# Gathering token rows in four pieces and turning them on VectorE; gate and up weights as one 8 KB run per partition

## What is computed

```python
scores = sigmoid(hf @ w_router)                  # 64 experts, 8 chosen for a token, weights sum to 2.5
hp = concatenate([hf, zeros((1, dm))])           # pad row
def body(acc, blk):                              # a block is 128 (token, expert) pairs of one expert
    toks, bw, e = blk
    xb = hp[toks]
    yb = (silu(xb @ w_gate[e]) * (xb @ w_up[e])) @ w_down[e]
    return acc.at[toks].add(yb * bw[:, None]), None
```

## Time and profile before

| | us |
|---|---|
| three runs | 2484.62, 2490.03, 2492.65 |
| median | 2490.03 |
| profiled execution | 2485.66 |
| its span, first to last instruction | 2483.8 |
| TensorE busy in the span | 2382.5 (96%) |
| VectorE busy | 1575.5 (63%) |
| ScalarE busy | 1161.9 (47%) |
| GpSimd busy | 767.3 (31%) |

### The profile page before, as it was taken

The page is one execution under the profiler, slowest core; times in us unless marked ns, Lnnn a source line. Parts: engine busy times, 40 slices in busy tenths (PEclk is TensorE's granted clock), DMA queues, the critical chain, the costliest instruction groups (busy, mean ns, idle before and its releaser), DMA issues. The chain is left out here.

```text
span 2483.8 us, 49979 instructions
## 1 busy us (share of the span) xinstructions
PE 2382.5 (96%) x11840; PEld 1954.7 (79%) x11842; DVE 1575.5 (63%) x2285; ACT 1161.9 (47%) x1621; POOL 767.3 (31%) x829
## 2 busy tenths in 40 slices
PE   8899999989997799999999999999999999999986
PEld 6677777678886688888888888888888888888875
DVE  6686867768878756555665555656665556655447
ACT  4525253542225645445554445545554445544334
POOL 0010100011110134334543433534443334444327
PEclk9999999989998899999999999999999999999998
DMA  7242323364445579778988878888888789987863
GB/s 254 77 144 98 111 94 111 117 218 164 171 164 206 196 230 284 223 219 270 273 259 233 254 218 263 268 266 262 257 253 243 224 223 274 283 247 222 216 221 136
DMA packets 253808, 524.34 MB, mean 211 GB/s; under 512 B 18065, under 2 KB 165169, under 8 KB 249649
## 3 DMA queue, kind: packets, MB, share of 16 engines
q1 hardware_dynamic: 204464, 336.64, 39.7%
q0 software_dynamic: 48672, 186.86, 29.4%
q10 hardware_dynamic: 608, 0.02, 0.0%
HBM read 386.61 MB, written 136.87 MB: 211 GB/s over the span
## 5 line engine op out<-in xcount | busy, mean ns | idle before, releaser
L2503 PE MATMUL psG<-gu_split,xT_hi 128*128 x2624 | 624.3, 390 | 2.9 <-ACT xT_hi L2340 1.5
L2503 PEld LDWEIGHTS psG<-gu_split,xT_hi 128*128 128x128 f32 x2624 | 493.8, 188 | 106.2 <-issue 3.6
L2326 POOL DMA_INDIRECT acc<-y,si x162 | 290.1, 1791 | 728.6 <-DMA acc<-y,si 413.3
L2409 DVE TENSOR_TENSOR gu_split<-raw_gu,gu_split (+1 forms) x127 | 290.6, 2288 | 175.3 <-ACT gu_split L2344 171.7
L2514 PE MATMUL psG<-gu_split,xT_lo 128*128 x1304 | 339.3, 402 | 5.9 <-issue 5.8
L2514 PEld LDWEIGHTS psG<-gu_split,xT_lo 128*128 128x128 f32 x1304 | 233.1, 188 | 50.1 <-issue 8.7
L2344 ACT ACTIVATE gu_split<-raw_gu x126 | 234.3, 1907 | 33.5 <-issue 33.5
L2301 POOL DMA_INDIRECT xg<-htab,gi x164 | 205.0, 1250 | 130.4 <-POOL gi L2298 109.7
L2409 DVE TENSOR_TENSOR d_lo<-raw_d,d_hi (+1 forms) x64 | 146.7, 2292 | 149.5 <-ACT d_hi L2344 149.5
L2389 ACT ACTIVATE HT_hi<-psH 128x256 fp32r<-128x256 f32 x162 | 62.4, 385 | 351.6 <-PE psH L2521 351.6
L2406 DVE TENSOR_TENSOR xT_lo<-psX,xT_hi 128x512 fp32r<-128x512 f32 x328 | 209.7, 680 | 8.5 <-ACT xT_hi L2340 8.5
(11 more groups left out here) (388 smaller groups left out, 3723.7 us busy)
## 6 DMA issues: line engine op xcount, KB each, us to landing
raw_gu<-in_w_gate_dram SPq DMA_DIRECT2D x64, 1024.0 KB, 6.0
raw_gu<-in_w_up_dram SPq DMA_DIRECT2D x64, 1024.0 KB
raw_d<-in_w_down_dram SPq DMA_DIRECT2D x64, 1024.0 KB, 6.9
wring<-split_d SPq DMA_DIRECT2D x24, 1024.0 KB, 4.8
split_d<-wring POOLq DMA_DIRECT2D x8, 1024.0 KB, 4.2
raw_d<-mixed SPq DMA_DIRECT2D x16, 512.0 KB, 3.9
xt<-in_x_dram SPq DMA_DIRECT2D x16, 512.0 KB, 4.3
htab<-h SPq DMA_DIRECT2D x16, 512.0 KB, 2.6
```

Of the source, the lines that this page charges most:

```text
L2326: nc.gpsimd.indirect_dma_start(out=acc, out_offset=bass.IndirectOffsetOnAxis(ap=si[k][:, 0:1], axis=0), in_=y[k][:], in_offset=None, compu ...
L2409: nc.vector.tensor_tensor(dst, src, hi, ALU.subtract).then_inc(dlo_s if n == 2 else gulo_s, 1)
L2503: nc.tensor.matmul(psG[slot][:], xT_hi[slot][:, c, :], right[:, bass.ds(w, 1), c, :].rearrange("p a n -> p (a n)"), start=(n == 0 and c == ...
```

## The change

1. htab becomes [rows, 4, 272]: piece a of a row is 256 floats of h and 16 routing weights. The writers of h and of the weights store piece by piece; the routing weights go out once per tile.
2. Each step gathers four times, 32 tokens by four pieces at a time: partition 32a + j of xg[:, g] gets piece a of token 32g + j. The row numbers 4 * token + a are made once in place_and_share (pidx, 16 small VectorE instructions).
3. VectorE turns xg in 32x32 squares to xF[:, c, :], c from 0 to 7, and the routing weights to xF[:, 8, :]. TensorE then turns only xF[:, 8, :], to psW, and pair_weight reads its column there. Column c of a partition p is row 8p + c of the matrix, so the gate and up weights are loaded as "(p k) n", 8 KB of one partition in one piece, each in its own half of the raw slot; their split goes by gate and up.
4. xT_hi is made from xF by one ScalarE instruction, xT_lo by one VectorE instruction. ScalarE makes gi and si, GpSimd only issues: four gathers and the scatter.
5. In a step VectorE runs HT_lo, pair_weight(n + 2), low_x(n + 3), product(n + 2), turn_x(n + 4), splits and y.

```diff
+def gather_pieces(nc, htab, to, at, done):
+    for g in range(QUADS):
+        nc.gpsimd.indirect_dma_start(out=to[:, g, 0:PIECE], out_offset=None, in_=htab.rearrange("r a w -> (r a) w"),
+                                     in_offset=bass.IndirectOffsetOnAxis(ap=at[:, g:g + 1], axis=0)).then_inc(done, 16)
...
+                dve.wait_ge(idx_s, 2)
+                for a in range(QUADS):
+                    for g in range(QUADS):
+                        last = nc.vector.tensor_scalar(pidx[a * QP:(a + 1) * QP, :, g], idx[g * QP:(g + 1) * QP, :], float(QUADS), float(a),
+                                                       ALU.mult, ALU.add)
...
-                    for w, sm, dst in ((w_gate, gate_in, wgu[:, s, :, 0:FE]), (w_up, up_in, wgu[:, s, :, FE:]),
+                    for w, sm, dst in ((w_gate, gate_in, runs_view(wgu)[:, s, 0]), (w_up, up_in, runs_view(wgu)[:, s, 1]),
...
-                    pool.wait_ge(turned[1], s.n + 3)
-                    pool.wait_ge(pairw_s, s.n + 3)
+                    pool.wait_ge(next_gi_s, s.n + 1)
                     carry_wait(pool, passed)
-                    gather(s.n + AHEAD, k, s.n + AHEAD + 1)
-                    nc.gpsimd.tensor_copy(si[k][:], idx[:, bass.ds(s.n, 1)]).then_inc(si_s, 1)
+                    gather_pieces(nc, htab, xg[k], gi[k], x_in[k])
...
+            def high_x(nth, slot):
+                act.wait_ge(turned_s, nth)
+                nc.scalar.activation(xT_hi[slot][:], xF[slot][:, 0:KC, :], ACT.Copy).then_inc(xhi_s, 1)
...
-                    evac_x(s.n + 3, k)
+                    high_x(s.n + 3, k)
+                    gather_index(s.n + AHEAD, k)
...
-                    act.wait_ge(added[k], s.turn * 16)
+                    scatter_index(s, k)
...
+            def turn_x(slot, gathered, ahead):
+                dve.wait_ge(x_in[slot], gathered * 16 * QUADS)
+                if ahead is not None:
+                    dve.wait_ge(wturn_s, ahead)
+                    dve.wait_ge(xhi_s, ahead)
+                carry_wait(dve, passed)
+                nc.vector.transpose(xF[slot][:, 0:KC, :].rearrange("p c (g j) -> p c g j", g=QUADS),
+                                    xg[slot][:, :, 0:D // QUADS].rearrange("p g (i c) -> p c g i", c=KC))
+                nc.vector.transpose(xF[slot][:, KC, :].rearrange("p (g j) -> p g j", g=QUADS),
+                                    xg[slot][:, :, D // QUADS:WIDE]).then_inc(turned_s, 1)
+
+            def low_x(nth, slot):
+                dve.wait_ge(xhi_s, nth)
+                nc.vector.tensor_tensor(xT_lo[slot][:], xF[slot][:, 0:KC, :], xT_hi[slot][:], ALU.subtract).then_inc(xlo_s, 1)
...
-                    for h in range(2):
-                        evac_x(h, s.n + 3, k)
                     s.wait(dve, H_s)
-                    pair_weight(nexts[n + 1], k, s.turn + 2)
+                    pair_weight(nexts[n], s.n + 2, 1 - k)
+                    low_x(s.n + 3, k)
                     product(s.n + 2, 1 - k)
+                    turn_x(1 - k, s.turn + k + 2, s.n + 2)
                     when_first(dve, nexts[n + 1], lambda: split(nexts[n + 1], 0))
...
+                nc.tensor.transpose(psW[:], xF[slot][:, KC, :], ident[:]).then_inc(wturn_s, 1)
...
-                    pe.wait_ge(x_in[1 - k], (s.turn + k + 2) * 16 )
-                    carry_wait(pe, passed)
-                    for h in range(2):
-                        pe.wait_ge(xlo_s[h], s.n + 3)
-                        turn_x(1 - k, h)
+                    turn_weights(s.n + 3, k)
...
-    htab = nc.dram_tensor("htab", [ROWS, ROW_W], F).ap()
+    htab = nc.dram_tensor("htab", [ROWS, QUADS, PIECE], F).ap()
```

More of the change, by code:

```diff
@@ L2128, in _, with load_expert, experts @@
                     down(n)
[L2131 to L2137, removed]
+def load_expert(eng, w_gate, w_up, w_down, expert, slot, wgu, wd, loaded, by_run=False):
+    gate, up = (runs_view(wgu)[:, slot, h] for h in range(2)) if by_run else (wgu[:, slot, :, 0:FE], wgu[:, slot, :, FE:])
+    for w, sm, dst in zip((w_gate, w_up, w_down), loaded, (gate, up, wd[:, slot])):
+        rows = "(p k) n -> p k n" if by_run and w is not w_down else "(k p) n -> p k n"
+        eng.dma_start(dst, w[0, expert].rearrange(rows, p=P)).then_inc(sm, 16)
+def experts(nc, passed, w_gate, w_up, w_down, ident, htab, acc, table, n_turns, idx, pidx, tails_s, xg, gi, gi_s, x_in, acc_out, gu, guhi_s, gulo_s, wgu, wd, loaded, y, si, added,
             prefetch_shared, prefetch_hT):
@@ L2160, in experts @@
         xT_lo = [sb(f"xT_lo{i}", [P, KC, P], FR) for i in range(2)]
+        xF = [sb(f"xF{i}", [P, KC + 1, P]) for i in range(2)]
         sg = sb("sg5", [P, FE])
@@ L2349, in _ @@
             pieces = list(parts(0, 1))
[L2350 removed]
+            high_x(1, 0)
             def split_gate_up(entry, before):
@@ L2483, in _, with turn_weights @@
         def _(pe):
-            def turn_x(slot, half):
-                for c in range(HALF):
-                    m = nc.tensor.transpose(psX[half][:, c, :], xg[slot][:, (half * HALF + c) * P:(half * HALF + c + 1) * P], ident[:])
-                m.then_inc(turned[half], 1)
+            def turn_weights(nth, slot):
+                pe.wait_ge(turned_s, nth)
+                if not (isinstance(nth, int) and nth == 1):
+                    pe.wait_ge(pairw_s, nth - 1)
+                carry_wait(pe, passed)
+                nc.tensor.transpose(psW[:], xF[slot][:, KC, :], ident[:]).then_inc(wturn_s, 1)
             def gate_up_high(nth, slot, entry):
-                for h in range(2):
-                    pe.wait_ge(xhi_s[h], nth)
+                pe.wait_ge(xhi_s, nth)
                 pe.wait_ge(gulo_s, entry.rank() * 2)
@@ L2535, in _ @@
             turn_H(0)
-            pe.wait_ge(x_in[0], 32)
-            for h in range(2):
-                pe.wait_ge(xlo_s[h], 2)
-                turn_x(0, h)
+            turn_weights(2, 1)
             def body(i):
```

158 lines of the change are left out of this document (82 added, 76 removed).

## The result

The changed kernel takes 2660.6 us (median of four runs, 2650.7 to 2671.7) against 2487.3 us for the kernel before on the same chip: a ratio of 1.0695, with the interval 1.0643 to 1.0747. It is slower by 173 us where the forecast, 2452 for the profiled execution of 2485.66, had it 34 us faster, and it lies 128 us beyond the slow end of the range. The profiled spans, 2664.3 and 2483.8 us, differ by 180.5 us.

The account below looks back on a forecast made before the run. TensorE was taken to set the pace, with the scatters' landing chain close behind. From 2485.7 us, minus 34 by that chain, minus 6 in the last nine steps, plus 6 at entry: 2452 us, range 2380 to 2533.

Parts of the forecast that it names:

- GpSimd's term: GpSimd's work per step: four gathers at 1.01 us each, 4.0 against 3.6 before; with the scatter 5.6 of 8.6 us.
- the sign that I had named for being wrong here: Gathers: the forecast is wrong if one of 272 floats does not take the time of one of 1088, 1.01 us.
- the chain of scatters: Each scatter waits for the previous landing; two-block experts go from 18.56 to 17.9 us, three-block from 27.84 to 27.4.
- VectorE's queue: VectorE in order: splits, y, the scatter and next HT_lo queue behind turn_x's wait for the gather; no time added.
- The sign that I gave: Trace sign of a right forecast: stalls on HT_lo or y behind a turn_x that waits for xg.
- VectorE's transpose: Turning 1024 columns on VectorE takes 1.25 us, bounds 1.22 to 2.44; VectorE then has 6.7 of 8.59 us.
- that rival: VectorE turns at half rate, 2.44 us per transpose: 2473 us in all, chance 0.12.
- TensorE's rival: TensorE stays the bound in the expert loop, with even steps near 8.6 us: 2381 us, chance 0.20.
- DMA: Landing of scatters with 8 KB weight and 1088-byte gather pieces: sum nothing, minus 2.4 to plus 0.4 us per long interval.
- Entry: Before the loop: pidx instructions, eight first gathers and two turns add 6 us, between 0 and 12.
- ScalarE at nothing: ScalarE has one xT_hi for two halves, plus two small copies: near 5 of 8.6 us, hidden behind TensorE, no cost.
- GpSimd's own sequence ends last (slower): Interval after the long one in two-block experts: 9.2 us instead of 8.2, +42 us, 2533 us in all, chance 0.23.

Follow-up runs that it names:

- e5: Changed kernel with one gather of whole rows plus three more gathers of 64 bytes per partition: 2625.3 us, ratio 1.0538.
- e7: Kernel before with each gather issued as four of 1088 bytes, TensorE still turning and weights in 1 KB pieces: 2675.9 us, ratio 1.0722.
- e4: Changed kernel with VectorE copying y before turn_x: 2600.4 us, ratio 1.0455.
- e3: Changed kernel with the transpose reading its squares from neighbouring floats instead of floats eight apart: 2623.5 us, ratio 1.0541.
- e12: Changed kernel with one gather of whole rows, squares from neighbouring floats, 1 KB gate and up pieces, and y ahead of turn_x: 2468.5 us, ratio 0.9923.
- e9: Kernel before with gate and up weights in 8 KB pieces, TensorE's transposes reading neighbouring columns: 2498.7 us, ratio 1.0055.
- e1: Changed kernel with gate and up weights in 1 KB pieces again: 2626.2 us, ratio 1.0559.
- e11: Kernel before with both index copies made by ScalarE instead of GpSimd: 2482.5 us, ratio 0.9976.
- e14: Changed kernel, four gathers kept, with 1 KB gate and up pieces, squares from neighbouring floats, and y ahead of turn_x: 2598.1 us, ratio 1.0438.
- e2: Changed kernel with one gather of whole 4352-byte rows per step, VectorE's turn kept: 2501.4 us, ratio 1.0051.
- e8: Kernel before with gate and up weights in 8 KB pieces, TensorE's transposes reading every eighth column: 2511.1 us, ratio 1.0072.

## Why the prediction was wrong

**The step that failed: "4.0 us against 3.6 before. With the scatter 5.6 of 8.6 us."** That is GpSimd's term. The duration of a short gather was right, 0.955 us for the 1.01 that I took, so the sign that I had named for being wrong here, a gather of 272 floats that takes another time, did not show. Missing were the gap of 0.30 before each gather (four times, 1.2 us), though I had counted the gaps of 0.79 and 0.90 of the copies that go; the stretch by VectorE's splits, which I named and did not put into the sum (mean 1.283 for 0.955, 1.3 us per step, read from the trace; no run takes the splits away); and the scatter's own 1.94 us and gap of 0.30 in place of 1.6. The 1.94 answers what no row showed of low_x: 61 of the 162 scatters meet none of VectorE's two-input subtractions and take 1.62 to 1.65 us, 65 meet low_x and take 1.91 at the median, 35 meet a split and take 2.54. By the page it is 4 x (1.283 + 0.30) + 1.94 + 0.30 = 8.6 us, where TensorE's step was to be 8.59. With no slack, each wait that GpSimd meets is added to the step, and the step came out at 10.37. e5 and e7 show that it is this term: three more instructions cost 124 us with the bytes of little more than one gather, and 185 us with TensorE turning. The condition was wrong as well: I held 5.6 against an average of 8.6, though the chain of scatters that I had read needs steps of 7.2 to 8.4 us between the long ones.

**VectorE's queue.** I wrote that "splits and y, and so the scatter and the next HT_lo" stand behind turn_x's wait, and priced it at nothing. Measured, the order costs 60 us in the kernel after (e4), net of the new waits that e4 makes. The sign that I gave, stalls on y behind a turn_x that waits for xg, is what the trace shows, at 350 us of waits.

**VectorE's transpose.** Taken 1.25, bounds 1.22 to 2.44; measured 2.12, near the upper one, and 1.24 without the step of eight floats (e3). The Trainium skill's one element per cycle per lane (Vector Engine (DVE) Microarchitecture Reference, The reshape front-end and per-opcode configuration) agrees with the 1.24 and not with the 2.12, and for a read with this step the measured 2.12 decides. The Trainium skill's penalty for each new 16-byte line (SBUF — State Buffer, Door 1: The DMA port swizzle) is the direction in which e3 differs; the runs do not show that it is the reason. In time it is 37 us in the kernel after, not the 21 that separated that rival from my forecast, but beside the gathers it is small.

**TensorE and the chain of scatters.** The time saved with the eight transposes is real, and so is a chain that takes most of it back: e12, with the gathers and the turn made cheap, is 21 us faster than the kernel before in the same set of runs, where the forecast said 34, and its scatters wait for landings as the forecast had them. e12 is the kernel nearest to what the forecast priced (though with one gather, 1 KB pieces and y ahead of the turn); the changed kernel is not. TensorE's rival of 2381 us falls with it.

**DMA.** Set to nothing, with bounds of minus 2.4 and plus 0.4 us per long interval. The weights' pieces are a loss of 9 to 14 us alone (e9) and 34 in the kernel after (e1). Why is not shown.

**Entry.** Forecast +6, bound +12; measured 13.7, the scatters' first start at 892.1 for 878.4. e7 has most of it, 891.3, from the four gathers and their row numbers alone.

**ScalarE at nothing** held in the main: it is busy 44% of the span, and e11 is faster for the copies it takes. But some 59 us of GpSimd's idle time before the scatters of the kernel after ended with these copies.

**The rival "GpSimd's own sequence ends last (slower)"** had the right place and sign and the wrong price: +42 us, by the interval after the long one at 9.2 us. In the timeline above the step filled by GpSimd alone takes 10.1, and the short intervals are gone throughout, 167 us in all. It should have led.

As a ladder, each step as measured: before 2490; copies on ScalarE 2482.5 (e11); the turn moved to VectorE and made cheap 2468.5 (e12); four gathers 2598 (e14); the turn at half rate and ahead of y and the 8 KB pieces 2660.6.

## What to carry to other kernels

An indirect gather costs its issuing engine by the instruction, not by the byte (0.95 us here for 64 as for 1088 bytes per row): add the gap before each one and the mean duration, not the median, and compare that sum, plus the waits that stand between these instructions in program order, with the new step and not with the old, and with its short steps, not with its average. When an engine at 40% gets four instructions for one, ask first whether it still has slack, and only then where the freed engine's time goes. A blocking wait moved to the head of an engine's queue has the price of everything behind it.

## What the runs showed of the hardware that I had not expected

- An indirect gather of 128 rows keeps GpSimd 0.95 us whether it brings 64 or 1088 bytes per row (medians 953 and 955 ns), and 0.98 to 1.01 us for 4352 in e2 and in the kernel before; 0.30 us passes before the next.
- VectorE's transpose of 1024 columns takes 1.24 us on neighbouring floats and 2.12 us with a step of eight; TensorE's weight load of a square takes 141 and 193 ns (e9, e8), its matmul 273 and 276.
- Weights in eight times larger pieces did not make a concurrent scatter land sooner at its worst: 12.2 us (e9) for 11.4 before.
